# Three of an expert's twelve weight units read by TensorE as plain fp32, the other nine split into a rounded part and a rest

## The reference, cut to what matters

```python
def expert_block(args):
    xb, e = args
    gu = xb @ w_gate_up[e] + b_gate_up[e]       # 64x1024 @ 1024x2048
    gl, up = jnp.split(gu, 2, axis=-1)
    gl = jnp.minimum(gl, SWIGLU_LIMIT)
    up = jnp.clip(up, -SWIGLU_LIMIT, SWIGLU_LIMIT)
    act = gl * jax.nn.sigmoid(SWIGLU_ALPHA * gl) * (up + 1.0)
    return act @ w_down[e] + b_down[e]          # 64x1024 @ 1024x1024
```

## Time and profile before

| what | value |
|---|---|
| time, median of 3 runs | 1992.04 us (1989.75 to 1992.68) |
| the profiled execution, first to last instruction (span) | 1987.6 us, 4.4 us under the median |
| mean granted TensorE clock, share of 2.4 GHz | 0.860 |
| PE busy | 1676.6 us, 84% |
| DVE busy | 1568.3 us, 79% |
| ACT busy | 1018.2 us, 51% |

### The profile page before, as it was taken

How to read it: one execution, slowest core, us unless ns; L and a number is a source line. 1 busy time by engine, 2 the same in 40 slices (tenths; PEclk the granted TensorE clock), 3 DMA queues, 4 the chain that set the end, 5 groups by cost and what they waited for, 6 DMA issues and landing times.

```text
span 1987.6 us, 22944 instructions
## 1 busy us (share of the span) xinstructions
PE 1676.6 (84%) x7686; PEld 1346.4 (68%) x7686; DVE 1568.3 (79%) x1568; ACT 1018.2 (51%) x931; POOL 287.4 (14%) x275
## 2 busy tenths in 40 slices
PE   6999968998989689897988888888979888888880
PEld 1888857457866567676777776776767677767760
DVE  1462599496373689998999989999989999899975
ACT  1222401211311346766767767767667677677651
POOL 1000075271060000101001001000010010010104
PEclk9899978999889758888888897988888888979885
DMA  9645411362405528899898998998998989989934
GB/s 336 223 150 142 149 43 43 114 191 77 169 0 233 205 89 345 333 379 373 332 373 360 355 372 342 368 379 330 380 370 336 372 354 353 378 340 369 381 116 180
DMA packets 120891, 533.38 MB, mean 268 GB/s; under 512 B 10064, under 2 KB 10576, under 8 KB 86544
## 3 DMA queue, kind: packets, MB, share of 16 engines
q1 hardware_dynamic: 112992, 506.58, 66.0%
q0 software_dynamic: 6640, 21.89, 3.4%
q10 hardware_dynamic: 1216, 4.33, 0.6%
HBM read 508.23 MB, written 24.54 MB: 268 GB/s over the span
## 4 chain that ended last, share of the span: by engine, by line
PE 43%; issue 7%; DVE 6%; ACT 5%; DMA 1%; POOL 0%; DVEq 0%; ACTq 0%; POOLq 0%
PE ps L728 24%; PE ps L751 16%; ACT stH L1002 4%; PE ps L738 3%; DVE workL L1433 2%; DVE AS L1487 1%; DVE hT L1476 1%; ACT G L1018 1%; DVE hT L1477 0%; DMA ring<-yrows_dram,rowi 0%; DVE work L332 0%; DVE hT L1482 0%; DVE hT L1479 0%; DMA yrows_dram<-qT 0%; POOL ring L1630 0%
## 5 line engine op out<-in xcount | busy, mean ns | idle before, releaser
L1433 DVE TENSOR_TENSOR ringL<-ring,stH 128x2048 fp32r<-128x2048 f32 x264 | 586.2, 2281 | 1.8 <-ACT stH L1002 1.8
L1002 ACT ACTIVATE stH<-ring 128x2048 fp32r<-128x2048 f32 x264 | 492.5, 1911 | 19.3 <-PE ps L751 18.0
L728 PE MATMUL ps<-stH,XS 128*128 128x512 f32 x1056 | 414.8, 393 | 6.1 <-DVE ringL L1433 5.9
L728 PE MATMUL ps<-ringL,XS 128*128 128x512 f32 x1056 | 416.4, 394 | 0.0
L751 PE MATMUL ps<-stH,AS 128*128 128x512 f32 x528 | 255.6, 484 | 128.9 <-DVE AS L1487 128.9
L1433 DVE TENSOR_TENSOR workL<-work,stH 128x2048 fp32r<-128x2048 f32 x132 | 301.4, 2283 | 51.4 <-ACT stH L1002 51.4
L1002 ACT ACTIVATE stH<-work 128x2048 fp32r<-128x2048 f32 x132 | 250.7, 1899 | 0.0
L751 PE MATMUL ps<-workL,AS 128*128 128x512 f32 x528 | 246.4, 467 | 0.0
L426 PE MATMUL ps<-hT,ring 128*128 128x264 f32 x1024 | 240.7, 395 | 0.0
L751 PEld LDWEIGHTS ps<-stH,AS 128*128 128x128 f32 x528 | 126.6, 240 | 164.5 <-DVE workL L1433 131.8
L728 PEld LDWEIGHTS ps<-stH,XS 128*128 128x128 f32 x1056 | 198.6, 188 | 51.8 <-issue 5.9
(11 more groups left out here) (357 smaller groups left out, 1825.2 us busy)
## 6 DMA issues: line engine op xcount, KB each, us to landing
ring<-gate_up_dram SPq DMA_DIRECT2D x264, 1024.0 KB, 11.3
work<-down_dram SPq DMA_DIRECT2D x132, 1024.0 KB, 6.5
ring<-in_dram SPq DMA_DIRECT2D x16, 2048.0 KB, 11.1
ring<-ada_dram SPq DMA_DIRECT2D x12, 2048.0 KB, 8.6
yrows_dram<-qT POOLq DMA_DIRECT2D x33, 256.0 KB, 6.7
yrows_dram<-S SPq DMA_DIRECT2D x1, 4096.0 KB, 20.5
ring<-pw_dram SPq DMA_DIRECT2D x2, 2048.0 KB, 7.7
ring<-out_dram SPq DMA_DIRECT2D x2, 2048.0 KB, 8.2
```

The lines of the kernel that those rows point to most:

```text
L728: mm = pe.matmul(bank(n), XS[:, i, :], part[:, n * 512:(n + 1) * 512], start=(i == 0 and a == 0), stop=(i == GU - 1 and a == 1))
L1002: act.activation(stH[:, i % NSTG, :], raw(i), ACT.Copy).then_inc(hi_done, 1)
L1433: dve.tensor_tensor(low(i), raw(i), stH[:, i % NSTG, :].bitcast(F32), ALU.subtract).then_inc(lo_done, 1)
```

## The change

The units 2 and 5 (gate and up) and 10 (down) are left whole (`WHOLE`). ACT makes no rounded copy of them and DVE no rest. PE reads the unit itself, `raw(i)`, as plain fp32, in four calls of 128x512 instead of eight, into the same banks between the other units. Its stationary operand is new: `XW` (for units 2 and 5) and `AW` (for the two halves of unit 10) hold 64 columns of unrounded rows, and 64 columns of zeros that POOL writes once. Both lie in the tile `row`. ACT fills `XW` ahead of `XS` and `AW` behind the rounded half of `AS`. PE waits for the load of a whole unit itself. The counts of `hi_done` and `lo_done` run over nine units; the count of units used still runs over twelve, so that ACT's wait for a slot of `stH` is what it was.

```diff
+WHOLE = (2, 5, 10)
+SPLIT = UNITS - len(WHOLE)
...
+        wide = row[:, :, :].rearrange("p a n -> p (a n)")[:, 0:4 * P].rearrange("p (i n) -> p i n", n=P)
+        XW, AW = wide[:, 0:2, :], wide[:, 2:4, :]
+        nth = lambda i: sum(u not in WHOLE for u in range(i))
...
                 for i in range(GU):
-                    pe.wait_ge(lo_done, UNITS * blk + i + 1)
+                    if i in WHOLE:
+                        pe.wait_ge(raw_in[i], 16 * blk + 16 + (RING_END if on_ring(i) else 0))
+                        for n in range(4):
+                            mm = pe.matmul(bank(n), XW[:, WHOLE.index(i), :], raw(i)[:, n * 512:(n + 1) * 512],
+                                           start=False, stop=(i == GU - 1))
+                        mm.then_inc(unit_used, 1)
+                        continue
+                    pe.wait_ge(lo_done, SPLIT * blk + nth(i) + 1)
...
                 for i in range(GU, UNITS):
-                    pe.wait_ge(lo_done, UNITS * blk + i + 1)
+                    if i in WHOLE:
+                        pe.wait_ge(raw_in[i], 16 * blk + 16 + (RING_END if on_ring(i) else 0))
+                        pe.wait_ge(aw_ready, blk + 1)
+                        for a in range(2):
+                            for n in range(2):
+                                mm = pe.matmul(bank(4 + n), AW[:, a, :], raw(i)[:, a * D + n * 512:a * D + (n + 1) * 512],
+                                               start=False, stop=False)
+                        mm.then_inc(unit_used, 1)
+                        continue
+                    pe.wait_ge(lo_done, SPLIT * blk + nth(i) + 1)
...
             def rows_hi(blk):
                 act.wait_ge(xt_done, blk + 1)
-                act.activation(XS[:, :, 0:CAP], ps[:, 0, :].rearrange("p (k n) -> p k n", k=KD), ACT.Copy).then_inc(xsh_ready, 1)
+                xt = ps[:, 0, :].rearrange("p (k n) -> p k n", k=KD)
+                if isinstance(blk, int):
+                    act.wait_ge(memset_done, 2)
+                act.activation(XW[:, :, 0:CAP], xt[:, WHOLE[0]:WHOLE[1] + 1:WHOLE[1] - WHOLE[0], :], ACT.Copy)
+                act.activation(XS[:, :, 0:CAP], xt, ACT.Copy).then_inc(xsh_ready, 1)
...
             def hi(blk, i):
 
+                if i in WHOLE:
+                    return
...
                 act.activation(AS[:, :, 0:CAP], nl[:, 2, :, :], ACT.Copy).then_inc(ash_ready, 1)
+                a0 = 2 * (WHOLE[2] - GU)
+                act.activation(AW[:, :, 0:CAP], nl[:, 2, a0:a0 + 2, :], ACT.Copy).then_inc(aw_ready, 1)
                 rows_hi(blk + 1)
...
             def lo(blk, i):
 
-                dve.wait_ge(hi_done, UNITS * blk + i + 1)
+                if i in WHOLE:
+                    return
+                dve.wait_ge(hi_done, SPLIT * blk + nth(i) + 1)
...
             pool.wait_ge(h2_ready, 1)
+            pool.memset(wide[:, :, CAP:], 0.0)
             pool.memset(r3[:, 0, :, :], 0.0)
```

More of the change, by code:

```diff
@@ L293, in build @@
         t1_ready = sem("t1_ready"); sg_ready = sem("sg_ready"); act_ready = sem("act_ready"); ash_ready = sem("ash_ready")
-        as_ready = sem("as_ready"); xt_done = sem("xt_done"); xsh_ready = sem("xsh_ready"); xs_ready = sem("xs_ready")
+        as_ready = sem("as_ready"); aw_ready = sem("aw_ready"); xt_done = sem("xt_done"); xsh_ready = sem("xsh_ready"); xs_ready = sem("xs_ready")
         idx_ready = sem("idx_ready"); xg_in = sem("xg_in"); yl_ready = sem("yl_ready"); y_ready = sem("y_ready"); y_out = sem("y_out")
```

## The result

The changed kernel takes 2101.51 us (median of 4 runs, 2100.16 to 2103.02), the kernel before 1992.36 us (4 runs, 1989.75 to 1993.03): a ratio of 1.0552, interval 1.0537 to 1.0567, so 109 us slower. The forecast was 2104 us.

The account below looks back on a forecast made before the run. PE's own loop, with one handover of AS from DVE in each of 33 blocks, was taken as the bound. Per block +4.8 - 1.4 = +3.4 us, so 1992.0 + 112 = 2104 us, range 2070 to 2155.

Parts of the forecast that it names:

- What PE pays for a whole unit: PE's units 2, 5, 10: plain records 0.43 us apart, 3.44 us a unit against 1.84 split, +4.8 us a block.
- What PE gets back: PE's wait for AS: without unit 10's split on DVE, AS comes earlier, 1.4 us a block.
- The clock: Units 8 to 11 on PE: the lower clock holds 4.8 us on the mean and keeps costing 2.4 us a block.
- The edits costed at nothing: AW and XW copies on ACT, slot and load waits, POOL's memset: all have cover and cost PE nothing.
- The sum: Whole kernel: +4.8 - 1.4 = +3.4 us a block, 33 blocks +112 us, 2104 us.
- cheap records: Rival on PE: a plain record costs no more than a split one, 0.23 us, giving 1946 us; 3 in 100.
- cheap calls: Rival on PE: a whole call takes one record's time, 1.72 us a unit, giving 1934 us; 2 in 100.
- the clock's recovery: Rival in units 8 to 11: the clock no longer falls after the shorter idle stretch, 2024 us; 7 in 100.
- its loss: Rival in units 8 to 11: the clock stays down longer, at most 2289 us; 8 in 100 for 2155 to this.
- one handover in each block: PE's wait for AS, 128.9 us in 33 blocks, is what PE lacks, not the amount of splitting.
- DVE was the bound after all: Rival: relieving DVE of 3 x 2.28 us a block pays; counted in the forecast's lower part, no chance of its own.
- A sign of it: Units 0 to 7 before the change: the last lo ended less than 2 us ahead of PE's turn for unit 7.

Follow-up runs that it names:

- e3: Changed kernel with plain fp32 calls of units 2, 5, 10 replaced by twice as many fp32r calls on neighbouring units' split parts, so products differ: 1939.45 us, ratio 0.9736.
- e5: Changed kernel plus one DVE subtraction of 128x2048 on a free stH slot, between the product and the rest half of AS: 2142.29 us, ratio 1.0758.
- e1: Changed kernel with unit 10 alone left whole, units 2 and 5 split as before, XW dropped: 2005.85 us, ratio 1.0068 to the kernel before.
- e2: Changed kernel with units 2 and 5 alone left whole, unit 10 split as before, AW dropped: 2084.40 us, ratio 1.0466 to the kernel before.
- e4: Kernel before, all units split, with DVE's split of unit 10 moved behind the rest half of AS: 1987.64 us, ratio 0.9985.
- e12: Kernel before with unit 10's DVE split behind the rest half of AS and ACT's rounded copy of unit 9 ahead of its copy to G: 1960.71 us, ratio 0.9846.

## Why the prediction was right

**What PE pays for a whole unit** was right in mechanism and size: 0.43 us between records, 3.43 us a unit, +3.18 us for two of them where 3.2 was forecast, and 162 us for all three by e3 where the terms gave 158 (9 of the 162 are the clock). That an instruction's price can be taken from another place in the same trace, with the same tile shape, is the step that carried the forecast.

**What PE gets back** was right in mechanism and a little large: 1.31 us over all blocks and 1.24 by e5, not 1.4, 3 to 5 us in all. The forecast took the gain from a block with the short fold, and in such a block it is exact: 10.67 to 9.25 us, 1.42. In 20 of 32 blocks of the changed kernel the fold and the transposes take some 3 us longer than in the earlier trace rows, at the lower clock, which uses up most of the wait.

**The clock** cost what it did in units 8 to 11, 4.66 us at 1.2 GHz against the 4.74 of before, but this was in part luck, for the reason given does not hold. The idle stretch ahead of unit 8 was to shrink to 3.6 us and stay the longest of the block; in 20 of 32 blocks it is 0.64 us, and the clock has fallen before it, in the fold. The block ahead in the earlier trace rows, with its transposes of 3.67 us, was one of those, and the prediction read it only for the idle time behind it. In such blocks the lower clock costs some 3 us in the fold and the transposes, a term that the sum doesn't have; the wait for `AS` hides most of it. And the term for units 8 to 11 does move with edits of this kind: 5.07 us in e1, 4.20 in e2, 4.12 in e3, that is 5 us more and 9 and 10 less in all. What decides where in a block the clock falls, no run here shows.

**The edits costed at nothing** had their cover. PE has one wait for a split of units 0 to 7, 5.9 us, as before, and none for a load or `AW` is among its waits. ACT does wait longer for slots of `stH`, behind the whole units; PE does not see it.

**The sum** landed 2.5 us from the median. The rivals fell: cheap records and cheap calls by e3, the clock's recovery and its loss by the stretches above.

One step was read wrongly, though it did not move the forecast. "It isn't the amount of splitting on DVE and ACT, busy as both are, that PE lacks; it is one handover in each block" holds only for the next 0.1 us: e4 removes the handover's delay and the block stops at 36.31 us, on DVE's splits. The rival "DVE was the bound after all" was dismissed because PE hardly waited for a split. DVE's loop, a tenth of a microsecond shorter than the one that rules, had left PE one long wait of this kind in all. A sign of it was in hand: the prediction noted that the last of the splits ended less than 2 us ahead of PE's turn for it. The changed kernel kept its 1.31 us, and the same edit also takes three subtractions off DVE: e4, with the earlier `AS` and all the splits, gained 4 us, e3, with the earlier `AS` and fewer splits, 53. So fewer splits were enough; whether PE's longer block would have been enough without them, no run shows.

## What to carry to other kernels

Before work is moved from helper engines to the one that sets the pace, price it there from a record of the same shape in the trace: here a plain fp32 unit costs 1.9 times a split one, and the 53 us that the helpers' relief gained could not pay for 162. A view of waits names the longest loop, not the second longest; lay out each engine's own loop over a block before you count on a wait's full length, as the two moved lines of e12 gave 30 us where the first of them alone gave 4. A small instruction in a busy engine's program can be held by its neighbour engine, so look at the shortest rows too after work has been moved to an idle engine. And where one piece of work has two lengths in one trace, look at the granted clock of both before anything else.

## What the runs showed of the hardware that was not expected

- A copy of 128x16 on DVE, 0.15 us, or 0.16, took 4.45 us beside POOL's subtraction, and so did a form with two inputs; a reduction from one input took 0.15 us. A step of the limits, 128x512, took 3.57 us beside it instead of 0.43. POOL's subtraction of 128x2048 took 4.52 us, DVE's 2.28.
- The lower clock fell in the fold in some blocks and behind it in others of the same kernel. The fold's 32 records took 3.79 us at a granted clock of 1.00 and 5.1 to 5.5 in the changed kernel's other blocks (0.67 in the one shown), the transposes 2.00 us at 1.00 and 3.67 at 0.50. Which of the two a block gets changed with small edits elsewhere: 20 of 32 blocks had the short fold before, 12 of 32 in the changed kernel.
